# Opening over a transposed w_ada: modulation columns as free-axis sums, the first two tiles projected block by block

## What is computed

```
mod = silu(c) @ w_ada + b_ada                 # c: 1024, w_ada: 1024 x 6144
shift1, scale1, gate1, shift2, scale2, gate2 = split(mod, 6)
h = rmsnorm(x, norm1_gain) * (1 + scale1) + shift1
proj = h @ w_in                               # 1024 x 1280: q 512 | k, v 256 | p 512
```

## Time and profile before

| | |
|---|---|
| median of 3 runs | 954.5 us (954.21 to 955.22) |
| span of the profiled execution | 952.9 us |
| PE busy | 927.6 us (97%) |
| DVE busy | 792.6 us (83%) |
| ACT busy | 512.9 us (54%) |
| POOL busy | 276.6 us (29%) |
| mean DMA rate | 204 GB/s |

### The profile page before, as it was taken

The page is one execution under the profiler, slowest core; times in us unless marked ns, Lnnn a source line. Parts: engine busy times, 40 slices in busy tenths (PEclk is TensorE's granted clock), DMA queues, the critical chain, the costliest instruction groups (busy, mean ns, idle before and its releaser), DMA issues.

```text
span 952.9 us, 14120 instructions
## 1 busy us (share of the span) xinstructions
PE 927.6 (97%) x4404; PEld 770.8 (81%) x4404; DVE 792.6 (83%) x1205; ACT 512.9 (54%) x980; POOL 276.6 (29%) x243
## 2 busy tenths in 40 slices
PE   4999999999999999999999999999999999999998
PEld 4887888878887777888888888888888888888886
DVE  7979999998689879797787977878798787977797
ACT  3247556676444747456464655546456464655543
POOL 0025554451100100704215070330705215070334
PEclk9999999999999999999999999999999999999999
DMA  9978453348255594655555555745655655555624
GB/s 355 399 236 285 159 197 117 109 156 279 96 155 173 176 340 150 245 206 213 209 187 221 176 185 211 263 140 184 224 215 206 211 191 215 177 188 208 220 88 177
DMA packets 96136, 193.97 MB, mean 204 GB/s; under 512 B 6513, under 2 KB 57441, under 8 KB 96097
## 3 DMA queue, kind: packets, MB, share of 16 engines
q1 hardware_dynamic: 90720, 182.02, 54.2%
q10 hardware_dynamic: 5376, 11.47, 3.5%
HBM read 176.30 MB, written 17.17 MB: 203 GB/s over the span
## 4 chain that ended last, share of the span: by engine, by line
PE 87%; DVE 5%; DMA 4%; ACT 2%; issue 1%; SPq 1%; POOL 0%; ACTq 0%; DVEq 0%; POOLq 0%
PE ps L2117 27%; PE ps L2119 27%; PE ps L2118 27%; DMA bs<-bs_scratch 2%; PE ps L2337 2%; DMA raw_u<-in_w_up 1%; PE ps L2216 1%; DVE acc L1360 1%; PE ps L2363 1%; PE ps L2227 1%; DMA ada_in_raw<-in_w_ada 1%; PE ps L2290 0%; DMA bs_scratch<-stg 0%; DMA m_raw<-mixed_scratch 0%; ACT qbd L832 0%
## 5 line engine op out<-in xcount | busy, mean ns | idle before, releaser
L1283 POOL TENSOR_TENSOR x<-x,p1s 128x512 f32<-128x512 f32 x80 | 116.0, 1470 | 422.0 <-ACT p1s L980 421.3
L2117 PE MATMUL ps<-bs,ring 128*128 128x512 f32 x344 | 134.4, 391 | 1.5 <-DVE h_lo L1724 0.7
L2119 PE MATMUL ps<-bs,ring 128*128 128x512 f32 x344 | 133.9, 389 | 0.0
L2118 PE MATMUL ps<-bs,ring 128*128 128x512 f32 x344 | 133.9, 389 | 0.0
L1731 DVE TENSOR_TENSOR ring<-s,ring 128x512 fp32r<-128x512 f32 x88 | 69.8, 811 | 50.3 <-ACT ring L901 50.2
L2117 PE MATMUL ps<-h_hi,ring 128*128 128x512 f32 x272 | 106.1, 390 | 0.5 <-DVE h_lo L1724 0.5
L2118 PE MATMUL ps<-h_lo,ring 128*128 128x512 f32 x272 | 105.8, 389 | 0.0
L2119 PE MATMUL ps<-h_hi,ring 128*128 128x512 f32 x272 | 105.8, 389 | 0.0
L901 ACT ACTIVATE ring<-s 128x512 fp32r<-128x512 f32 x88 | 53.8, 623 | 66.5 <-PE ps L2119 66.5
L2117 PEld LDWEIGHTS ps<-bs,ring 128*128 128x128 f32 x344 | 64.6, 188 | 16.9 <-DMA bs<-bs_scratch 1.9
L2119 PEld LDWEIGHTS ps<-bs,ring 128*128 128x128 f32 x344 | 64.6, 188 | 13.5
(11 more groups left out here) (291 smaller groups left out, 2333.9 us busy)
## 6 DMA issues: line engine op xcount, KB each, us to landing
bs<-bs_scratch SPq DMA_DIRECT2D x166, 512.0 KB, 6.2
stage<-in_w_ada SPq DMA_DIRECT2D x24, 512.0 KB, 5.9
raw_g<-in_w_gate SPq DMA_DIRECT2D x11, 1024.0 KB, 5.2
raw_u<-in_w_up SPq DMA_DIRECT2D x11, 1024.0 KB, 7.4
raw_d<-in_w_down SPq DMA_DIRECT2D x20, 512.0 KB, 4.1
ada_in_raw<-in_w_ada SPq DMA_DIRECT2D x16, 512.0 KB, 12.4
wi_raw<-in_w_in SPq DMA_DIRECT2D x8, 640.0 KB, 15.3
wo_raw<-in_w_out SPq DMA_DIRECT2D x8, 512.0 KB, 5.7
```

Source lines behind the costliest of these rows:

```text
L1283: pool.tensor_tensor(x1_half(t, 1), x1_half(t, 1), p1s[j][:, :], ALU.add).then_inc(pool_evac, 1)
L2117: pe.matmul(dst, s_hi, m_hi, start=start, stop=False, skip_group_check=onto)
L2118: pe.matmul(dst, s_hi, m_lo, start=False, stop=False, skip_group_check=onto)
L2119: return pe.matmul(dst, s_lo, m_hi, start=False, stop=stop, skip_group_check=onto)
```

## The change

The host gives w_ada a second time, transposed (in_w_adat, 6144 x 1024). A 512 KB piece of it holds 128 output columns on partitions and all 1024 inputs along the free axis. PE transposes silu(c), broadcast, into a row that stands on all partitions (crow), and DVE forms one block of a modulation vector by one multiply with a sum over the free axis (column_sum), in place of folds, transposes and reductions. SCALE1, SHIFT1, SCALE2 and SHIFT2 go this way; GATE1 and GATE2 stay folds. sum_columns at it 4 and 6 goes away.

- Tiles 0 and 1 are no longer scaled as a whole: ACT's h_high_block takes the high part of x * a1 of one block of both tiles (256 columns), with a1 as the scale; DVE's h_low_block subtracts. shift_high and shift_low work on one block (128 columns) each.
- SP loads block by block: scale piece j, w_in block j, and from j = 2 on shift piece j - 2 behind a wait for a1_done. The table's two loads move from ACT's queue to SP's.
- ACT's vrow loads are split in two groups: norm1_gain and b_ada first (with vcol_done 1 behind them), seven others later. small_vectors holds what is left of the small copies and the write of the table to scratch; it comes behind wi_high(2). constants holds the read back and the constants' loads; it comes behind wi_high(4), ahead of shift_high(1).
- PE projects block j of tile 0 and of tile 1, then from j = 3 on the shift product of block j - 3. Of block 7 it does tile 0, tile 1's kv, shift blocks 4 to 7, and last tile 1's q and p.
- In it 0, h_low(2) follows evac_q(0), and scale_x(3) and fold(0) move behind the v copies. ACT keeps all three parts of the shift product before square_qk(0). sh_hi and sh_lo move out of the load buffers; xt 2 gets a buffer of its own (sq_m); w_out's first loads no longer wait for shift_ps.

The diff, cut to what orders the work:

```diff
+            sp.dma_start(vrow[0:KT, :], c[0].rearrange("(r p) -> r p", p=P)).then_inc(c_in, 16)
...
+            def load_scale(j):
+                sp.dma_start(first_view(j), wat_d[SCALE1 * D + j * P:SCALE1 * D + (j + 1) * P, :]).then_inc(ada_in[j], 16)
+            def load_shift(j):
+                sp.wait_ge(a1_done, j + 1)
+                sp.dma_start(first_view(j), wat_d[SHIFT1 * D + j * P:SHIFT1 * D + (j + 1) * P, :]).then_inc(ada_in[j], 16)
+            def load_wi(j):
+                sp.dma_start(wi_raw[:, j, :], win_d[j * P:(j + 1) * P, :]).then_inc(piece_in[j], 16)
             def load_xt(t):
-                sp.dma_start(xs[:, t % 2], xt[t]).then_inc(xt_in[t % 2], 16)
-            for k in range(KT):
-                load_first(0, SCALE1, k)
+                sp.dma_start(xs_of(t), xt[t]).then_inc(xt2_in if t == 2 else xt_in[t % 2], 16)
+            load_scale(0)
             load_xt(0)
-            for j in range(KT):
-                sp.dma_start(wi_raw[:, j, :], win_d[j * P:(j + 1) * P, :]).then_inc(piece_in[j], 16)
+            load_wi(0)
             load_xt(1)
-            sp.wait_ge(acc1_done, 2)
-            for k in range(KT):
-                load_first(1, SHIFT1, k)
...
+            sp.dma_start(onehot_sb, onehot).then_inc(table_in, 16)
+            sp.dma_start(table_sb, rel_bias_table).then_inc(table_in, 16)
+            for j in range(1, KT):
+                load_scale(j)
+                load_wi(j)
+                if j >= 2:
+                    load_shift(j - 2)
+                if j == 5:
+                    sp.dma_start(x_st[:, :], x_d[0:P, :]).then_inc(x_in, 16)
+            load_shift(KT - 2)
+            load_shift(KT - 1)
+            sp.wait_ge(rel_done, 1)
             load_xt(2)
-            sp.wait_ge(hlo_done, 2)
-            load_xt(3)
...
-            sp.wait_ge(mod_done, 2)
+            sp.wait_ge(hlo_done, KT + 1)
+            load_xt(3)
+            sp.wait_ge(shift_sum, KT)
...
-                sp.dma_start(piece_view(n), wa_d[k * P:(k + 1) * P, mm * D:(mm + 1) * D]).then_inc(stage_in[n % RING], 16)
+                src = wa_d[k * P:(k + 1) * P, mm * D:(mm + 1) * D] if mm == GATE1 else wat_d[mm * D + k * P:mm * D + (k + 1) * P, :]
+                sp.dma_start(piece_view(n), src).then_inc(stage_in[n % RING], 16)
                 if (mm, k) == (GATE1, KT - 1):
-                    sp.wait_ge(shift_ps, 3)
...
+                act.wait_ge(small_ps, 5)
+                act.activation(rel_sb, bank(6)[0:NQ, 0:3 * CHUNK], ACT.Copy).then_inc(rel_done, 1)
+                act.wait_ge(rel_done, 1)
+                act.dma_start(rel_dram, rel_sb.unsqueeze(1).broadcast_to([NQ, CHUNK, 3 * CHUNK])).then_inc(rel_out, 16)
+            def constants():
+                act.wait_ge(rel_out, 16)
+                for h in range(2):
+                    act.dma_start(bias[h * CHUNK:(h + 1) * CHUNK, 0],
+                                  bass.AP(rel_dram.tensor, h * CHUNK * 3 * CHUNK + CHUNK - 1,
+                                          [[3 * CHUNK - 1, CHUNK], [2 * CHUNK * 3 * CHUNK, NPR], [1, P]])).then_inc(bias_in, 16)
+                act.dma_start(invc[:, :, :], inv_count.partition_broadcast(P)).then_inc(const_in, 16)
+                act.dma_start(wpl[:, :, :], w_pool[0].rearrange("g c d -> c g d")).then_inc(const_in, 16)
+                act.dma_start(psc_bc, pool_scale[0].rearrange("(g d) -> g d", g=NP).partition_broadcast(P)
...
+                with nc.allow_non_contiguous_dma(reason="eight sinks"):
+                    for h in range(2):
+                        act.dma_start(sinks[h * HD:(h + 1) * HD, :],
+                                      attn_sinks[0].rearrange("(r h) -> h r", h=2)[h].partition_broadcast(HD)
+                                      ).then_inc(const_in, 16)
...
+            wi_high(0, slice(0, QW))
+            h_high_block(0, 0, 1)
+            act.activation(crow[:, :], ps[:, 0:2, :].rearrange("p a b -> p (a b)"), ACT.Copy).then_inc(crow_done, 1)
+            wi_high(0, slice(QW, IN))
+            h_high_block(0, 1, 2)
+            for j in range(1, KT):
+                h_high_block(j, 0, 2)
                 wi_high(j)
-            act.wait_ge(rel_done, 1)
-            act.dma_start(rel_dram, rel_sb.unsqueeze(1).broadcast_to([NQ, CHUNK, 3 * CHUNK])).then_inc(rel_out, 16)
-            h_high(1)
...
+                if j == 2:
+                    small_vectors()
+                if j == 4:
+                    constants()
+                if j >= 3:
+                    shift_high(j - 3)
             square_x(0)
+            for j in range(KT - 3, KT):
+                shift_high(j)
...
+            def column_sum(piece, row, v, j):
+                return dve.scalar_tensor_tensor(out=piece, in0=piece, scalar=1.0, in1=row, op0=ALU.mult, op1=ALU.mult,
+                                                accum_out=mod_sum[:, v, j:j + 1])
...
-                    ins = dve.tensor_scalar(a, piece_view(n), cact[:, 0, 0:1], None, ALU.mult)
+                if mm != GATE1:
+                    ins = column_sum(piece_view(n), crow[:, :], {SCALE2: 2, SHIFT2: 3}[mm], k)
...
-                dve.wait_ge(mod_done, v + 1)
+            def scale_column(j):
+                dve.wait_ge(ada_in[j], 16)
+                if j == 0:
+                    dve.wait_ge(small_ps, 3)
+                elif j == 1:
+                    dve.wait_ge(crow_done, 1)
+                row = ps[:, 0:2, :].rearrange("p a b -> p (a b)") if j == 0 else crow[:, :]
+                link(column_sum(first_view(j), row, 0, j))
+                dve.tensor_scalar(a1[:, j:j + 1], mod_sum[:, 0, j:j + 1], b1[:, j:j + 1], vcol[:, N1 + j:N1 + j + 1],
+                                  ALU.add, ALU.mult).then_inc(a1_done, 1)
...
-            take_first(0, (0, 1))
-            gain_columns(a1, 0, N1)
-            dve.wait_ge(xt_in[0], 16)
-            scale_x_first(0, xs0_first)
-            wi_low(0)
-            h_low_first(0, hhi0_first, hlo0_first)
-            scale_x_first(1, xs_done)
-            wi_low(1)
-            h_low_first(1, hhi_done, hlo_done)
-            for j in range(2, KT):
+            dve.wait_ge(vcol_done, 1)
+            link(dve.tensor_scalar(b1[:, :], vcol[:, BA + SCALE1 * KT:BA + (SCALE1 + 1) * KT], 1.0, None, ALU.add))
+            scale_column(0)
+            wi_low(0, slice(0, QW), 0)
+            h_low_block(0, 0, 1)
+            wi_low(0, slice(QW, IN))
+            h_low_block(0, 1, 2)
+            for j in range(1, KT):
+                scale_column(j)
+                if j >= 3:
+                    shift_column(j - 3)
+                h_low_block(j, 0, 2)
+                if j >= 3:
+                    shift_low(j - 3)
                 wi_low(j)
-            scale_x(1)
-            h_low(1)
-            fold_first(1)
-            take_first(1, (5, 6))
-            shift_low(0)
-            shift_low(1)
+            for j in range(KT - 3, KT):
+                shift_column(j)
+                if j > KT - 3:
+                    shift_low(j - 1)
             scale_x(2)
-            h_low(2)
...
                     m_low(2)
                 if it == 0:
-                    fold(0)
                     evac_q(0)
-                    scale_x(3)
+                    h_low(2)
...
                 if it == 0:
+                    scale_x(3)
+                    fold(0)
...
+            pe.wait_ge(vrow_in, 16 * 2)
+            pe.transpose(bank(7)[:, 0:N2], vrow[0:N2, :], ident[0:N2, 0:N2]).then_inc(small_ps, 1)
+            pe.wait_ge(cact_done, 1)
+            for k in range(KT):
+                last = pe.transpose(bank4(k // 4)[:, k % 4, :], cact[:, 0, k:k + 1].broadcast_to([P, P]), ident[:, :])
+            last.then_inc(small_ps, 1)
             pe.wait_ge(set_pool, 1)
-            for k in range(2, KT):
-                pe.wait_ge(ada_in[k], 16)
-                keep_busy(2)
-            transpose_sums(0, (0, 1))
-            keep_busy(10)
+            keep_busy(8)
+            pe.wait_ge(piece_in[0], 16)
+            keep_busy(4)
+            def small_vectors():
+                pe.wait_ge(vrow2_in, 16 * 7)
+                pe.wait_ge(vcol_done, 1)
+                pe.transpose(bank(7)[:, N2:NV], vrow[N2:NV, :], ident[N2:NV, N2:NV]).then_inc(small_ps, 1)
+                pe.wait_ge(table_in, 32)
+                pe.matmul(bank(6)[0:NQ, 0:3 * CHUNK], table_sb, onehot_sb, start=True, stop=True).then_inc(small_ps, 1)
+            Q_COLS, KV_COLS, P_COLS = slice(0, QW), slice(QW, QW + KVW), slice(QW + KVW, IN)
...
+                for j in range(KT - 1):
+                    project_block(0, j)
+                    project_block(1, j)
+                    if j == 1:
+                        small_vectors()
+                    if j >= 3:
+                        if j == 3:
+                            pe.wait_ge(vcol_done, 2)
+                            pe.wait_ge(rel_done, 1)
+                        for part in range(3):
+                            shift_part(part, (j - 3,))
```

(12 more changed lines are left out.)

339 lines of the change are left out of this document (131 added, 208 removed).

## The result

The changed kernel takes 972.79 us (median of 4 runs, 971.71 to 972.88), the kernel before beside it 954.64 (954.21 to 955.22): ratio 1.0187, 95% interval 1.0173 to 1.0202. That is 18.1 us slower, where 11.0 were forecast, and above the end of the range at 970. The profiled execution has a span of 971.0 us against 952.9. TensorE's row answers to the earlier trace rows: the same busy time and a granted clock that is no longer full everywhere.

A forecast was written before the change was run, and what follows sets the result against it. PE, busy 97%, was taken as the bound, so only its waits or removed work could win, chiefly the opening. Scores 12.6 us late, minus 2, plus 0.4 gave +11.0: span 963.9, time 965.5 us, range 960 to 970.

The forecast's parts named there:

- the step on which it rested: Opening: scratch write lands at 38.2 us, ACT stalls from 29.4, block 4 ready at 45.7, PE loses 13 us; chance 0.58.
- rival 2: Scratch write in the opening: queues take equal turns, it lands at 32.2 us, everything 6 us earlier, 959.5 us; chance 0.12.
- The blocks' period: Opening, blocks from 3 on: DVE needs 5.1 us a block, PE 5.2, DMA 4.1, a balanced pipeline.
- the start: Opening: tile 0's first projection matmul starts at 12 us instead of 21.56.
- the clock: After the opening's stall: PE slow again following 13 us of idleness, up to 2 us, taken as 1.
- Up to evac_q(0): Opening through the shift product's q part: evac_q(0) starts at 69.1 us instead of 57.22, 11.9 late.
- 0.7 more: From evac_q(0) to first scores: DVE gains h_low(2) 1.2 and fold(0) 0.75 us, less waits lost; scores 12.6 us late.
- loses most of the 1.5 us of waits: DVE between evac_q(0) and scores: its added work mostly replaces 1.5 us of waits before ss_qk and the scores.
- I take 2: Mixing phase: SCALE2 and SHIFT2 sums leave PE, 3.5 us for two; between 0 and 3.5 come back, taken as 2.
- 0.4 lost: Mixing phase: sixteen column sums carry the accumulator output, 0 to 2.7 us, taken as 0.4 net of links that fall away.
- Rival 3: Opening: the write has landed when ACT asks, only issues remain, block 4 ready at 36.7, 955.5 us; chance 0.13.
- Rival 4: Opening: wait and issues both covered, PE bounds from block 3, scores 1.5 us early, 951 us; chance 0.13.

The follow-up runs named there:

- a1: Changed kernel with constants() (wait and seven DMA issues) moved from behind wi_high(4) to behind the block loop, ahead of square_x(0): 962.59 us, ratio 1.0087.
- a2: Changed kernel with the wait for the scratch write left behind wi_high(4) and only the seven DMA issues moved behind the loop: 970.67 us, ratio 1.0166.
- a4: Changed kernel with 56 useless 128-column matmuls behind shift block 0 to keep TensorE busy in the gap: 971.59 us, ratio 1.0172.
- b4: Changed kernel with constants on SyncE, plus fold(1), bias tiles and fold(2) behind it 0's norms and evacuations: 969.24 us, ratio 1.0152.
- e1: Changed kernel with constants on SyncE, third and fourth x tiles loaded earlier, eight one-column matmuls at it 4 and 6, folds and h_low(3) behind norms: 959.91 us.
- c2: c1 plus eight unused one-column matmuls at mixing steps 4 and 6, as many records as the removed sums had: 960.81 us, ratio 1.0074.
- c1: Changed kernel with constants on SyncE and the third x tile's load ahead of the last two shift loads: 961.75 us, ratio 1.0081.
- b3: Kernel before with the transposed w_ada as a further input, of which 4 KB are read once: 957.16 us, ratio 1.0024.
- a3: Changed kernel with the scratch write cut from 64 to 8 copies (64 packets), the read back taking its first row: 966.03 us, ratio 1.0119.
- d4: c2 with the fourth x tile's load ahead of the constants and the transposed w_ada declared last: 960.26 us, ratio 1.0071.
- b2: Changed kernel with constants on SyncE, plus sixteen unused one-column matmuls at mixing steps 4 and 6: 973.06 us, ratio 1.0214.

## Why the prediction was right and wrong

**Right: the step on which it rested.** Write issued until 23.0 us (forecast 23.6), first bias load out at 38.76 (38.2), block 4's low part ready at 45.4 (45.7), TensorE's gap 12.7 us (13). a1 and a2 show that the gap is this stall: without the wait and the issues it is gone, with the wait alone it is 8.2 us. The landing came within 0.6 us of its forecast, since the write got the same small share of the DMA as in the earlier trace rows. The rule of equal turns (rival 2) would have had the load out at 32.2; 1323 packets against 520 speak against it again. They speak only against equal turns by the profile's packets (3.9 KB each on SP's queue, 0.75 KB in the write); turns by larger units are not excluded. The blocks' period was 5.24 us (5.1), the accumulator's read 0.08 us (0.1), the start 10.5 us (12).

**Wrong: three terms behind it**, 7.1 us in all. The waits behind evac_q(0) and the gain of the removed sums failed as steps, the clock in its size, and for the FFN's start there was no term.

1. *Up to evac_q(0):* +13.4 for +11.9. The lower clock was put at 1 us; a4 shows about 2.4. The steps' slips make the rest.
2. *evac_q(0) to the scores, "0.7 more":* measured 2.6. VectorE's further work was sized right (1.9 us forecast; without its waits this stretch grew from 14.6 to 16.3 us, 1.7). What failed is "loses most of the 1.5 us of waits": these two, for ScalarE's sq_qk and TensorE's scores, grew from 1.0 to 1.3 and from 0.4 to 1.3 us, and all waits of the stretch from 2.2 to 3.1. TensorE ran dry for 4.7 us in front of the norms and did the scores' preparation on a lower clock (0.64 from 85 to 90 us). I take that for the cause of the second wait, from the order of the rows; no run isolates it. b4 and e1 show that a wait goes from one engine to the next when it is pushed.
3. *Later, "I take 2" back and 0.4 lost:* measured a loss of 2.1. The offset fell by 1.1 us by it 6 (16.0 to 14.9), but not through the removed sums: it falls as much in c2, which has them back (4.9 to 3.7). The removal gained nothing there and cost 0.9 us at it 7, half of the +1.8, by a collision of POOL and VectorE that it brought about itself; c2 against c1 shows it. What makes the offset fall by it 6 and the other half of the rise stays open. A further 1.4 us came at the FFN's start; b3 shows the same slower stores in the kernel before with only a further input and one small load of it. The prediction had no step for either, and its range ended at the sum of the bounds of steps that it had.

Rival 3 deserves a note: its price was wrong. With the landing out of the way (a3) the time is 966.0 and not 955.5. Of these 10.5 us some 2.5 are the longer issues (7.7 us for 5.2) and 2.4 the lower clock, which it left out; most of the rest are the terms 2 and 3 above, which it shared with the forecast. Rival 4 (951) had the q part of the shift product end at 53.9 us; the opening alone comes near that (evac_q(0) at 56.0 us in c1, 54.7 in d4), but the scores are then 4.9 and 3.4 us late instead of 1.5 early.

## What to carry to other kernels

A wait on an in-order engine is priced by what stands behind it, and the landing of a small transfer by its packets and the share that it gets beside a busy queue, not by the full rate of the DMA: both can be read off the trace before anything is changed. When work is taken off an engine, ask which others then meet: an engine that hands over earlier can start a third one in the middle of a fourth one's costliest instructions. And a stall early on is not only shifted to the end; each stretch whose engines were in step before has to be priced again.

## What the runs showed of the hardware that was not expected

- The issue of the same seven DMAs on ScalarE's queue took 4.4 us (changed kernel), 5.4 (a4), 6.5 (a1) and 7.7 us (a3); the two loads of sinks alone 1.29 to 3.86 us.
- A small copy of POOL (64 columns, 0.27 us in the changed kernel) took 2.86 us in the kernel before and 1.86 in c2 where it met VectorE's instructions with two SBUF inputs in mid-run. In the changed kernel, where it came while the first of them ran, POOL's sums and VectorE's instructions both ran slower instead (2.02 for 1.14 us, 8.05 for 6.02).
- A further kernel input, 4 or 24 MB, declared first or last, together with one 4 KB load of it, raised the issue of eight 256 KB stores to DRAM from 0.67 to 0.87 us each and cost 2 us; a scratch tensor of 24 MB did not. Input and additional load were not separated.
- In b2, the second row of 32 one-column records (3.63 us, from 192.35 us on) was followed by a granted clock of 0.52 (near the 1.2 GHz level), nine matmuls 0.43 us apart instead of 0.23. Behind the first such row (3.63 us, from 146.43 us on) and behind rows of sixteen, in the kernel before and in c2, the clock stayed at full speed.
